# Two-block model on one core: the first block's attention output made by feature, with two steps moved

## The chip, the core and the metric

The kernel runs on one core of one Trainium2 chip. The metric is the device time of one execution in microseconds, lower is better. The engines are named as in the profile: PE is TensorE (PEld its weight loads), DVE is VectorE, ACT is ScalarE, POOL is GpSimd, SP is the queue that fetches the weights.

## What is computed

A model of two blocks of two layers each over 256 tokens of width 1024. Only the two layers of the first block are touched, and in them the attention branch, whose weights come from a softmax over keys that an index score has picked:

```
def dsa_attention(q, k, v, qi, ki, wi):
    ...
        q_g = q_b.reshape(bsz, Q_BLOCK, A_KV_HEADS, group, A_HEAD_DIM)
        s = jnp.einsum('btngd,btknd->btngk', q_g, k_g).astype(jnp.float32) * scale
        s = jnp.where(valid[:, :, None, None, :], s, -jnp.inf)
        p = jax.nn.softmax(s, axis=-1).astype(v.dtype)
        o = jnp.einsum('btngk,btknd->btngd', p, v_g)
        return o.reshape(bsz, Q_BLOCK, A_WIDTH)
...
def rwkv7_time_mix(z, mu, w0, w_up, a0, a_up, g_up, k_k, k_a, r_k, ln_w, ln_b):
    ...
    kk = (kf * k_k.astype(f32)).reshape(hs)
    kk = kk * lax.rsqrt(jnp.maximum(jnp.sum(kk * kk, axis=-1, keepdims=True), 1e-24))
    ...
        sa = jnp.einsum('bhvk,bhk->bhv', state, ka_t)
        state = (state * w_t[:, :, None, :] + sa[..., None] * kb_t[:, :, None, :]
                 + v_t[..., None] * k_t[:, :, None, :])
```

The second function is a recurrence over time. The kernel works it in four chunks of 64 tokens, and for that needs the inverse of a triangular matrix for each chunk and head. A layer adds three gated branches (attention, a short convolution, the recurrence), projects them, and ends in a feed-forward part.

## The kernel before

Every matrix product with weights is made of three matmuls on rounded parts: ACT rounds a slab of 128x2048 weights into `w_high` (step `round`, L596), DVE subtracts to get `w_low` (step `split`, L978), and PE multiplies high by high, high by low and low by high (L1499 to L1501). There are three slabs and three pairs of parts, so slab u is rounded once the products of slab u-3 are done. A slab's work is a *unit*: `uc` 0 to 3 and `cb` 0 and 1 feed the convolution branch, `ga` and `gb` 0 to 3 the gates of the first two branches, `br0` the projection of the attention output, and so on in the order of `UNITS_A`. Between units each engine does the steps that `schedule_a` hangs on them. All engines walk the same list in order, each doing its own part of a step, and wait for each other by semaphores; there is no scheduler.

Attention goes by pairs of heads k = 0 to 3, spread over seven host units (`rz` 6, `uc` 0 to 3, `cb` 0 and 1): at host n come `scores` of pair n, `turn` of pair n-2 (six transposes of the exponentials through banks 5 and 6, copied out by ACT) and `pv` of pair n-3. `pv` multiplies the transposed exponentials as weights (128 columns) by 64 columns of values: six matmuls with tokens on the output's partitions, each of which the profile lists as two records, since they are in full f32. DVE divides by the softmax sums as it empties bank 7 (L1271, L1273). Later, behind unit `ga` 2, `post` 0 and 1 transpose the outputs to features by tokens in banks 6 and 7 (L1877), and ACT and DVE make the high and low part that `br0` needs, both reading the bank (DVE at L1281).

In the same stretch the recurrence is prepared. Behind `uc` 3 PE spreads the inverse of the keys' norm over the heads' rows (`kk_spread`, L1912) and DVE scales the keys (`kk_scale`, L1309), scans the decays (L1291) and, behind `cb` 0, makes the scaled keys (`keys`, L1325 to L1331). PE makes the chunks' Gram matrices (`chunk`, L1948) and DVE masks them (`mask`, L1344). From here a serial chain runs beside PE's gate units: ACT writes the diagonal blocks out (`blocks_out`, L893), POOL reads them and inverts them by 15 steps of two small tensor ops (`invert`, L2185 and L2187), writes the inverses (L2191), makes the off-diagonal part and shifts a bias (`off_diag` L2197, `bonus_shift` L2153), and then issues eight DMAs that bring the transposed inverses back (`blocks_in`, L2161); ACT issues eight for the inverses themselves (L902). The first product of `solve` 0 on PE (L1994), behind unit `gb` 3, waits for POOL's eight.

The arena is an SBUF buffer for everything between; `bank` is PSUM.

Of the kernel before, what the change touches and what calls it, by code (L numbers as in the profile page):

```python
# [11 lines left out]
F32 = mybir.dt.float32  # L12
F32R = mybir.dt.float32r
I32 = mybir.dt.int32
ALU = mybir.AluOpType
# [290 lines left out]
def stage_starts():  # L306
# [14 lines left out]
    dve_emptied3=10, dve_emptied4=6, dve_emptied5=10, dve_emptied6=8, dve_emptied7=6, exps=4, g_made=2,  # L321
# [4 lines left out]
    normed=4, off_diagonal=1, outputs_turned=2, products=84, qk_raw=6, queries_ready=1, rate_made=2,  # L326
    reset_made=1, rest_copied=18, rhs_made=4, rooted=1, rooted_sums=2, roped=6, row_kept=1, sa_made=4,
    scored=4, silu=22, solved=8, spread_made=4, squared=8, state=3, state_made=3, summed=8, summed_decay=2,
    tok_made=6, tokens_scaled=1, transposes_in=128, turned=8, u_made=3, up_scaled=22, weighted=4, x_high=12,
    x_ready=12, y_made=4, y_rooted=1, y_scale=1, y_squared=2, y_variance=1, ya_done=2, ya_high=2, yb_high=2,  # L330
    yb_ready=2, yc=2, yc_high=2, yc_ready=2, z_mixed=7,), "b": dict(
# [83 lines left out]
def schedule_a(first):  # L415
# [22 lines left out]
    for n, unit in enumerate(hosts):  # L438
        put(unit, *([("conv", n - 1)] if 1 <= n < 5 else []), *([("lora_inputs", 0)] if n == 2 else []))
        work = [(name, n - lag) for name, lag in (("pv", 3), ("turn", 2), ("scores", 0)) if 0 <= n - lag < 4]  # L440
        put(unit, *(work + [ROUND_NEXT] if unit == ("uc", 3) else [ROUND_NEXT] + work))
    amid(("uc", 3), ("lora", 0), ("kk_inverse", 0))
    put(("uc", 3), ("kk_spread", 0), ("kk_scale", 0), ("blend", 0), ("decay", 0), ("blended", 0))
# [224 lines left out]
def scalar_a(core, eng, line, stage):  # L668
# [159 lines left out]
    def post(n):  # L828
        eng.wait_ge(*sem("outputs_turned").next(eng))
        act(core.xh[:, 2 * n:2 * n + 2, :], heads(bank[6 + n], T), ACT.Copy, sem("ya_high"))  # L830
# [222 lines left out]
def vector_a(core, eng, line, stage):  # L1053
# [212 lines left out]

    def pv(k):
        eng.wait_ge(*sem("weighted").upto(k + 1))
        rden = core.small[:, RDEN_:RDEN_ + 4]
        line.settled()  # L1270
        did(eng.reciprocal(rden, core.small[:, DEN_ + 4 * (k % 4):][:, 0:4]))  # L1271
        line.settled()
        did(tt(flat(core, OS_, 4).rearrange("p (m c) -> p m c", m=2)[:, :, P * k:P * k + P].rearrange("p m (h d) -> p m h d", h=2),  # L1273
               bank[7][:, 0:T].rearrange("p (m h d) -> p m h d", m=2, h=2),
               rden.rearrange("p (m h) -> p m h", m=2).unsqueeze(3).broadcast_to([P, 2, 2, HD]), ALU.mult),
            sem("dve_emptied7"))

    def post(n):
        b = 6 + n
# [1666 lines left out]
```

## Time and profile before

| | us |
|---|---|
| median of 3 runs | 1671.35 |
| lowest and highest of the 3 | 1671.22, 1672.12 |
| the profiled execution's own time | 1670.61 |
| its span, first to last instruction | 1668.1 |
| PE busy in the span | 1654.6 |
| DVE busy | 1195.6 |
| ACT busy | 971.6 |
| POOL busy | 213.4 |

A row of the timeline gives start, length, engine, line, operation, what it writes and reads, partitions and columns, the number of records, and in square brackets how long the engine had been idle and who released it. The length of a merged PE row includes the time in which the last result leaves the array, so the pace is read from start to start.

### The profile page before, as it was taken

Reading aid. Unit: us, or ns where it says so; the run is one execution under the profiler, and the core shown is the slowest. Engines: PE = TensorE matmul, PEld = TensorE weight load, DVE = VectorE, ACT = ScalarE, POOL = GpSimd, SP = SyncE. Lnnn points to the kernel's source line nnn. Section 1 sums busy time; section 2 is a strip of 40 time slices with the busy share of each in tenths; the row PEclk is TensorE's granted clock in tenths of the full one; section 3 lists DMA queues with packets and bytes.
Section 4 is the critical chain, followed back from the end, with each engine's and each line's share of the span. In section 5 each row is a group of like instructions: output and inputs, shape, how many; then the busy total and the mean of one; then the engine's idle time right before and its main releaser. Section 6 shows DMA issues by size and latency. Waiting matters only on the chain.

```text
span 1668.1 us, 29334 instructions
## 1 busy us (share of the span) xinstructions
PE 1654.6 (99%) x12160; PEld 1473.4 (88%) x12160; DVE 1195.6 (72%) x1676; ACT 971.6 (58%) x1483; POOL 213.4 (13%) x208
## 2 busy tenths in 40 slices
PE   9999999999999999999999999999999999999998
PEld 6999999999998999999999998778788987788887
DVE  7877547798888975548888875767756657677564
ACT  7674525565567565345555564666774556657743
POOL 1764500000002945100000000000000100000000
PEclk9999999999999999999999999999999999999999
DMA  7443523454545424525454445334445553443451
GB/s 263 152 152 113 185 103 125 180 202 177 188 160 196 158 102 148 166 92 191 155 204 176 185 178 187 142 128 175 140 167 180 183 189 131 148 175 128 169 185 51
DMA packets 48195, 268.14 MB, mean 161 GB/s; under 512 B 13568, under 2 KB 14464, under 8 KB 16448
## 3 DMA queue, kind: packets, MB, share of 16 engines
q1 hardware_dynamic: 38160, 263.65, 44.0%
q10 hardware_dynamic: 9136, 1.58, 0.5%
q8 instruction: 96, 1.57, 0.4%
q0 software_dynamic: 768, 1.05, 0.2%
q14 instruction: 35, 0.29, 0.1%
HBM read 264.42 MB, written 1.84 MB: 160 GB/s over the span
## 4 chain that ended last, share of the span: by engine, by line
PE 58%; DVE 1%; DMA 0%; ACT 0%; POOL 0%; issue 0%; DVEq 0%; ACTq 0%
PE bank L2662 11%; PE bank L2664 11%; PE bank L2663 10%; PE bank L1499 4%; PE bank L1500 4%; PE bank L1501 4%; PE bank L1552 4%; PE bank L1554 2%; PE bank L2692 2%; PE bank L2680 1%; PE bank L2724 1%; PE bank L2711 1%; PE bank L1046 1%; PE bank L2702 0%; PE bank L1638 0%; PE bank L1996 0%
## 5 line engine op out<-in xcount | busy, mean ns | idle before, releaser
L978 DVE TENSOR_TENSOR w_low<-slab,w_high 128x2048 fp32r<-128x2048 f32 x249 | 577.8, 2330 | 200.4 <-ACT w_high L596 193.5
L596 ACT ACTIVATE w_high<-slab 128x2048 fp32r<-128x2048 f32 x249 | 470.2, 1896 | 115.8 <-PE bank L2664 71.8
L1499 PE MATMUL bank<-act,w_high 128*128 128x256 f32 (+1 forms) x1744 | 501.9, 288 | 0.9 <-DVE w_low L978 0.8
L1500 PE MATMUL bank<-act,w_high 128*128 128x256 f32 (+1 forms) x1744 | 493.2, 283 | 0.0
L1501 PE MATMUL bank<-act,w_low 128*128 128x256 f32 (+1 forms) x1744 | 493.1, 283 | 0.0
L1499 PEld LDWEIGHTS bank<-act,w_high 128*128 128x128 f32 (+1 forms) x1744 | 332.8, 191 | 10.8 <-issue 5.6
L1500 PEld LDWEIGHTS bank<-act,w_high 128*128 128x128 f32 (+1 forms) x1744 | 333.1, 191 | 0.9 <-issue 0.5
L1501 PEld LDWEIGHTS bank<-act,w_low 128*128 128x128 f32 (+1 forms) x1744 | 333.0, 191 | 0.0
L2662 PE MATMUL bank<-w_high,act 128*128 128x512 f32 x768 | 305.7, 398 | 0.0
L2664 PE MATMUL bank<-w_low,act 128*128 128x512 f32 x768 | 299.7, 390 | 0.0
L2663 PE MATMUL bank<-w_high,act 128*128 128x512 f32 x768 | 299.3, 390 | 0.0
L1552 PE MATMUL bank<-act,w_high 128*128 128x512 f32 x576 | 204.4, 399 | 0.0
L2217 POOL TENSOR_TENSOR arena<-arena 128x512 f32<-128x512 f32 x8 | 14.4, 1798 | 1286.6 <-ACT arena L621 1286.6
L2662 PEld LDWEIGHTS bank<-w_high,act 128*128 128x128 f32 x768 | 144.3, 188 | 31.9 <-issue 3.7
L2664 PEld LDWEIGHTS bank<-w_low,act 128*128 128x128 f32 x768 | 144.2, 188 | 31.0
L2663 PEld LDWEIGHTS bank<-w_high,act 128*128 128x128 f32 x768 | 144.4, 188 | 28.1
L672 ACT ACTIVATE arena<-bank 128x512 f32<-128x512 f32 (+4 forms) x158 | 77.2, 499 | 154.2 <-PE bank L1554 44.9
L1554 PE MATMUL bank<-act,w_low 128*128 128x256 f32 x576 | 161.8, 281 | 0.0
L1552 PEld LDWEIGHTS bank<-act,w_high 128*128 128x128 f32 x576 | 108.3, 188 | 26.1
L1554 PEld LDWEIGHTS bank<-act,w_low 128*128 128x128 f32 x576 | 108.9, 189 | 0.0
L2290 ACT ACTIVATE arena<-bank,small 128x512 f32<-128x512 f32 x80 | 54.9, 686 | 83.3 <-PE bank L2664 82.2
L1148 DVE SCALAR_TENSOR_TENSOR arena<-arena,vectors 128x255 f32<-128x255 f32 (+1 forms) x176 | 85.1, 483 | 12.4 <-ACT arena L672 3.6
(261 smaller groups left out, 1850.8 us busy)
## 6 DMA issues: line engine op xcount, KB each, us to landing
slab<-stream_a SPq DMA_DIRECT2D x143, 1024.0 KB, 4.8
slab<-stream_b SPq DMA_DIRECT2D x104, 1024.0 KB, 4.7
residual<-x_t SPq DMA_DIRECT2D x4, 256.0 KB, 6.2
slab<-stream_a ACTq DMA_DIRECT2D x2, 512.0 KB, 5.7
lora_weights<-lora SPq DMA_DIRECT2D x2, 512.0 KB, 7.5
out_t<-residual SPq DMA_DIRECT2D x4, 256.0 KB, 2.3
d_inverse<-arena POOLq DMA_DIRECT2D x2, 256.0 KB, 2.3
constants<-common SPq DMA_DIRECT2D x1, 384.0 KB, 9.1
```

Source lines behind the costliest of these rows:

```text
L596: line.did(eng.activation(core.wh[u % PARTS][:, 0:SLAB_WIDTH[u]], core.slab[u % SLABS][:, 0:SLAB_WIDTH[u]], ACT.Copy), core.sem("slab_high"))
L672: line.did(eng.activation(out, in_, func, **kw), tally)
L978: line.did(line.eng.tensor_tensor(core.wl[u % PARTS][:, 0:SLAB_WIDTH[u]], core.slab[u % SLABS][:, 0:SLAB_WIDTH[u]], core.wh[u % PARTS][:, ...
L1148: did(stt(out=out[:, lag:T], in0=src[:, 0:T - lag], scalar=col("conv", 2 * FT * tap + half * FT + j), in1=out[:, lag:T], op0=ALU.mult, op1 ...
L1499: eng.matmul(out, wh, xh, start=first, stop=False, skip_group_check=True)
L1500: eng.matmul(out, wh, xl, start=False, stop=False, skip_group_check=True)
L1501: return eng.matmul(out, wl, xh, start=False, stop=last, skip_group_check=True)
L1552: eng.matmul(out[:].rearrange("p (n t) -> p n t", n=2), wh[:, k, j, :], core.x[:, :, at, :], start=k == 0, stop=False, skip_group_check=True)
L1554: return eng.matmul(out[:, 0:T], wl[:, k, j, :], core.xh[:, at, :], start=False, stop=k == 7, skip_group_check=True)
L2662: mm(bank[b][:], high, wh[:, k, :], start=(half == 0 and k == 0), stop=False, skip_group_check=True)
L2663: mm(bank[b][:], low, wh[:, k, :], start=False, stop=False, skip_group_check=True)
L2664: last = mm(bank[b][:], high, wl[:, k, :], start=False, stop=(half == 1 and k == 3), skip_group_check=True)
```

## The change

`pv` now uses the values as weights (64 columns) and lets the transposed weights of the softmax stream through, in a helper that the second block already uses (`pe_weighted`): four matmuls instead of six, with features on the output's partitions. Nothing has to be transposed afterwards, so PE has no `post` step any more. The division by the softmax sums can no longer be done on the output (tokens are now its columns), so DVE does it ahead of the transposes, on the exponentials, in a new step `share` (`dve_share`: a reciprocal of 128x4 and two multiplications in the arena, of 128x2x128 and 128x2x256), one host behind `scores`. `turn` waits for `shared` instead of `exps`. `pv` on DVE is a plain copy of 128x256, and `post` on ACT and DVE reads the arena instead of the banks. Two steps move: `kk_spread` goes ahead of `turn` 2 on PE, and at host `cb` 0 ACT does the copies of `turn` 3 ahead of rounding the next slab.

```diff
@@ schedule_a
-        work = [(name, n - lag) for name, lag in (("pv", 3), ("turn", 2), ("scores", 0)) if 0 <= n - lag < 4]
-        put(unit, *(work + [ROUND_NEXT] if unit == ("uc", 3) else [ROUND_NEXT] + work))
+        work = [(name, n - lag) for name, lag in (("pv", 3), ("turn", 2), ("scores", 0), ("share", 1)) if 0 <= n - lag < 4]
+        if n == 4:
+            work.insert(1, ("kk_spread", 0))
+        put(unit, *(work + [ROUND_NEXT] if n in (4, 5) else [ROUND_NEXT] + work))
...
-    put(("uc", 3), ("kk_spread", 0), ("kk_scale", 0), ("blend", 0), ("decay", 0), ("blended", 0))
+    put(("uc", 3), ("kk_scale", 0), ("blend", 0), ("decay", 0), ("blended", 0))
@@ ACT
     def post(n):
-        eng.wait_ge(*sem("outputs_turned").next(eng))
-        act(core.xh[:, 2 * n:2 * n + 2, :], heads(bank[6 + n], T), ACT.Copy, sem("ya_high"))
+        eng.wait_ge(*sem("outputs_kept").upto(2 * n + 2))
+        act(core.xh[:, 2 * n:2 * n + 2, :], core.a(OS_ + 2 * n, 2), ACT.Copy, sem("ya_high"))
@@ DVE
+    def share(k):
+        eng.wait_ge(*sem("exps").upto(k + 1))
+        dve_share(core, line, k, scores_of(core, k, ASC_), sem("shared"))
+
     def pv(k):
         eng.wait_ge(*sem("weighted").upto(k + 1))
-        rden = core.small[:, RDEN_:RDEN_ + 4]
-        line.settled()
-        did(eng.reciprocal(rden, core.small[:, DEN_ + 4 * (k % 4):][:, 0:4]))
-        line.settled()
-        did(tt(flat(core, OS_, 4).rearrange("p (m c) -> p m c", m=2)[:, :, P * k:P * k + P].rearrange("p m (h d) -> p m h d", h=2),
-               bank[7][:, 0:T].rearrange("p (m h d) -> p m h d", m=2, h=2),
-               rden.rearrange("p (m h) -> p m h", m=2).unsqueeze(3).broadcast_to([P, 2, 2, HD]), ALU.mult),
-            sem("dve_emptied7"))
+        did(eng.tensor_copy(flat(core, OS_ + k), bank[7][:, 0:T]), sem("dve_emptied7"))
+        line.tell(sem("outputs_kept"))
 
     def post(n):
-        b = 6 + n
-        eng.wait_ge(*sem("ya_high").next(eng))
-        did(tt(core.xl[:, 2 * n:2 * n + 2, :], heads(bank[b], T), core.xh[:, 2 * n:2 * n + 2, :].bitcast(F32), ALU.subtract),
-            sem(f"dve_emptied{b}"))
-        line.tell(sem("ya_done"))
+        low(2 * n, 2, core.a(OS_ + 2 * n, 2), "ya_high", "ya_done")
@@ PE
     def turn(k):
-        eng.wait_ge(*sem("exps").upto(k + 1))
+        eng.wait_ge(*sem("shared").upto(k + 1))
...
     def pv(k):
         eng.wait_ge(sem("act_emptied5").sem, turn.at[k])
-        p_t = turned_of(core, k, APT_)
         banks.fill(7, "dve")
-        for m in range(2):
-            for p in range(2):
-                for s in range(m + 1):
-                    n = 2 * m + p * (m + 1) + s
-                    ins = mm(bank[7][:, (2 * m + p) * HD:][:, 0:HD], p_t[:, n * P:n * P + P],
-                             half_of(core, WS_, s)[:, P + HD * p:P + HD * p + HD], start=(s == 0), stop=(s == m),
-                             skip_group_check=True)
-        ins.then_inc(sem("weighted").sem, 1)
-
-    def post(n):
-        if n == 0:
-            eng.wait_ge(sem("dve_emptied7").sem, banks.count[7, "dve"])
-        b = 6 + n
-        banks.fill(b, "dve")
-        for j in range(2):
-            for m in range(2):
-                ins = eng.transpose(bank[b][:, j * T + m * P:][:, 0:P], half_of(core, OS_, m)[:, T * n + P * j:][:, 0:P],
-                                    core.const("ident"))
-        ins.then_inc(sem("outputs_turned").sem, 1)
+        pe_weighted(eng, bank[7], turned_of(core, k, APT_),
+                    lambda t, p: half_of(core, WS_, t)[:, P + HD * p:P + HD * p + HD]).then_inc(sem("weighted").sem, 1)
```

PE at host `uc` 3, before: the last product of the unit, `pv` 1 (L1865), `turn` 2 (L1852), `kk_spread` (L1912), and the first product of `cb` 0.

```order
L1501 MATMUL bank<-act,w_low 128x256
L1865 MATMUL bank<-arena 128x64 x6
L1852 MATMUL bank<-constants,arena 128x128 x6
L1912 MATMUL bank<-arena,constants_a 128x256 x4
L1499 MATMUL bank<-act,w_high 128x256
```

The same place after the change (L1048 and L1051 are `pe_weighted`, L1890 is `kk_spread`, L1848 `turn`).

```order
L1497 MATMUL bank<-act,w_low 128x256
L1048 MATMUL bank<-arena 64x256 x2
L1051 MATMUL bank<-arena 64x128 x2
L1890 MATMUL bank<-arena,constants_a 128x256 x4
L1848 MATMUL bank<-constants,arena 128x128 x6
L1495 MATMUL bank<-act,w_high 128x256
```

Six matmuls have become four, and the spread stands ahead of the transposes.

DVE from the split of host `uc` 2 to the scan, before: L1303 inverts the keys' norms, L1187 empties `uc` 3's bank, then come `pv` 1, `kk_scale` (L1309), a small op for `blend` and the scan.

```order
L978 TENSOR_TENSOR w_low<-slab,w_high 128x2048
L1303 RECIPROCAL arena<-arena 128x256
L1187 TENSOR_TENSOR arena<-bank,arena 128x256
L1271 RECIPROCAL small<-small 128x4
L1273 TENSOR_TENSOR arena<-bank,small 128x2x128
L1309 TENSOR_TENSOR arena<-bank,arena 128x512 x2
L1313 TENSOR_SCALAR small<-vectors 128x4
L1291 SCALAR_TENSOR_TENSOR arena<-arena 128x1024
```

The same place after the change, with `share` 2 ahead of the split (L980) and `share` 3 (L1033, L1037) ahead of `kk_scale` (L1305).

```order
L1033 RECIPROCAL small<-small 128x4
L1037 TENSOR_TENSOR arena<-arena,small 128x2x128
L1037 TENSOR_TENSOR arena<-arena,small 128x2x256
L980 TENSOR_TENSOR w_low<-slab,w_high 128x2048
L1299 RECIPROCAL arena<-arena 128x256
L1189 TENSOR_TENSOR arena<-bank,arena 128x256
L1275 COPY arena<-bank 128x256
L1033 RECIPROCAL small<-small 128x4
L1037 TENSOR_TENSOR arena<-arena,small 128x2x128
L1037 TENSOR_TENSOR arena<-arena,small 128x2x256
L1305 TENSOR_TENSOR arena<-bank,arena 128x512 x2
L1309 TENSOR_SCALAR small<-vectors 128x4
```

Two multiplications inside the arena now stand between the copy of `pv` 1 and `kk_scale`.

DVE from the last masks to the gate units, before: masks, `keys` 1, a split, the two low parts of `post` (L1281), the splits of the next slabs.

```order
L1344 TENSOR_TENSOR arena<-bank,constants_a 128x512 x4
L1335 TENSOR_TENSOR arena<-bank,arena 128x512 x2
L978 TENSOR_TENSOR w_low<-slab,w_high 128x2048
L1281 TENSOR_TENSOR act<-bank,act 128x512 x2
L978 TENSOR_TENSOR w_low<-slab,w_high 128x2048 x6
```

After the change:

```order
L1340 TENSOR_TENSOR arena<-bank,constants_a 128x512 x4
L1331 TENSOR_TENSOR arena<-bank,arena 128x512 x2
L980 TENSOR_TENSOR w_low<-slab,w_high 128x2048
L1114 TENSOR_TENSOR act<-arena,act 128x512 x2
L980 TENSOR_TENSOR w_low<-slab,w_high 128x2048 x6
```

The order is the same; the two low parts now have both inputs in SBUF.

## Rows read from the trace of the kernel before

**Rows 1.** The page's busy time: us, share of the span, instructions.

```profile
PE 1654.6 (99%) x12160; PEld 1473.4 (88%) x12160; DVE 1195.6 (72%) x1676; ACT 971.6 (58%) x1483; POOL 213.4 (13%) x208
```

**Rows 2.** Waits of PE: us in total, times, longest.

```profile
PE bank L1877 <- ACT arena L672: 2.2, 2, 1.1
...
PE bank L1994 <- DMA arena<-d_inverse: 0.6, 1, 0.6
```

**Rows 3.** Timeline of PE in the first layer, host uc 2.

```profile
104.82 1.45 PE L1865 MATMUL bank<-arena 128*128 128x64 f32 x12
106.10 0.83 PE L1852 MATMUL bank<-constants,arena 128*128 128x128 f32 x6
```

**Rows 4.** Timeline of PE in the second block, the helper `pe_weighted` there.

```profile
1449.51 0.65 PE L1046 MATMUL bank<-arena 128*64 128x256 f32 x4
...
1450.31 0.66 PE L2738 MATMUL bank<-constants,arena 128*128 128x128 f32 x4
```

**Rows 5.** Timeline of PE in the first layer, from `post` 0 to unit ga 3.

```profile
163.03 0.60 PE L1877 MATMUL bank<-constants,arena 128*128 128x128 f32 x4
...
165.13 0.36 PE L1499 MATMUL bank<-act,w_high 128*128 128x256 f32 x1
```

**Rows 6.** Timeline of PE in the first layer, `solve` 0.

```profile
195.57 2.08 PE L1994 MATMUL bank<-arena 64*64 64x64 f32 x64 [0.55 <-DMA arena<-d_inverse]
```

**Rows 7.** Timeline of ACT and POOL: the chain's first DMAs and its last.

```profile
154.07 5.33 ACTq L893 DMA_DIRECT2D d_blocks<-arena  x8
...
185.89 4.50 POOL L2161 DMA_DIRECT2D arena<-d_inverse  x8
```

**Rows 8.** Timeline of DVE in the first layer, behind unit uc 3.

```profile
117.36 0.42 DVE L1187 TENSOR_TENSOR arena<-bank,arena 128x256 f32<-128x256 f32 x1 [3.46 <-ACT arena L672]
...
118.88 1.29 DVE L1309 TENSOR_TENSOR arena<-bank,arena 128x512 f32<-128x512 f32 x2 [0.36 <-PE bank L1912]
```

**Rows 9.** Timeline of DVE in the second block: both multiplications of one `dve_share`.

```profile
1053.80 1.02 DVE L1035 TENSOR_TENSOR arena<-arena,small 128x256 f32<-128x256 f32 x2
```

**Rows 10.** Timeline of POOL in the first layer: a free operation, and four of the chain.

```profile
142.62 2.23 POOL L2143 TENSOR_TENSOR arena<-arena,vectors 128x1024 f32<-128x1024 f32 x1
...
169.44 2.23 POOL L2185 TENSOR_TENSOR arena<-arena 128x64 f32<-128x64 f32 x1
171.75 0.32 POOL L2187 TENSOR_TENSOR arena<-arena 128x64 f32<-128x64 f32 x1
...
178.55 3.49 POOL L2197 TENSOR_TENSOR arena<-arena,constants_a 128x1024 f32<-128x1024 f32 x1
182.00 3.94 POOL L2153 TENSOR_TENSOR arena<-arena,vectors 128x1024 f32<-128x1024 f32 x1
```

**Rows 11.** Timeline of DVE, three of the splits beside that chain.

```profile
169.21 2.29 DVE L978 TENSOR_TENSOR w_low<-slab,w_high 128x2048 fp32r<-128x2048 f32 x1 [0.76 <-ACT w_high L596]
...
180.46 3.73 DVE L978 TENSOR_TENSOR w_low<-slab,w_high 128x2048 fp32r<-128x2048 f32 x1 [0.69 <-ACT w_high L596]
186.22 2.29 DVE L978 TENSOR_TENSOR w_low<-slab,w_high 128x2048 fp32r<-128x2048 f32 x1 [2.02 <-ACT w_high L596]
```

**Rows 12.** Timeline of ACT, a gate's sigmoids ahead of a rounding.

```profile
183.54 0.84 ACT L672 ACTIVATE arena<-bank,vectors 128x256 f32<-128x256 f32 x2 [3.11 <-PE bank L1501]
```

**Rows 13.** L2161's DMAs issued from 187 to 188, and from 189 on.

```profile
DMA to landing us min/median/max: 2.4/2.6/3.0
...
DMA to landing us min/median/max: 5.7/5.8/5.8
```

**Rows 14.** Busy time of stretches at the kernel's end; PEclk is the granted clock.

```profile
1659.00:1660.00 1.00, 1.00 (x11) 1.00 (x10) 0.00 (x0) 0.81 (x3) 0.00 (x0) 1.00 0.00 0
...
1661.00:1662.00 1.00, 0.40 (x1) 0.41 (x2) 0.51 (x3) 0.00 (x0) 0.00 (x0) 0.50 0.00 0
```

**Rows 15.** Timeline of PE: the opening burst, and the same shape later.

```profile
1.31 7.25 PE L2077 MATMUL bank<-arena 128*128 128x512 f32 x12 [1.31 <-POOL arena L2226]
...
154.59 1.98 PE L1931 MATMUL bank<-arena,constants 128*128 128x512 f32 x4
```

More of the change, by code:

```diff
@@ L320 @@
     convolved=22, decay_made=2, decays=1, diagonal=2, dve_emptied0=20, dve_emptied1=10, dve_emptied2=19,
-    dve_emptied3=10, dve_emptied4=6, dve_emptied5=10, dve_emptied6=8, dve_emptied7=6, exps=4, g_made=2,
+    dve_emptied3=10, dve_emptied4=6, dve_emptied5=10, dve_emptied6=7, dve_emptied7=5, exps=4, g_made=2,
     gate_input=1, gathered=3, hidden=22, hidden_high=22, hidden_low=22, index_scores=4, index_summed=4,
@@ L325 @@
     lora_out=2, masked=1, maxed=4, mean_square=2, mix_high=4, mix_ready=4, newest_tap=22, norm_spread=2,
-    normed=4, off_diagonal=1, outputs_turned=2, products=84, qk_raw=6, queries_ready=1, rate_made=2,
+    normed=4, off_diagonal=1, outputs_kept=4, products=84, qk_raw=6, queries_ready=1, rate_made=2,
     reset_made=1, rest_copied=18, rhs_made=4, rooted=1, rooted_sums=2, roped=6, row_kept=1, sa_made=4,
[L328 to L331, printed above, removed]
+    scored=4, shared=4, silu=22, solved=8, spread_made=4, squared=8, state=3, state_made=3, summed=8,
+    summed_decay=2, tok_made=6, tokens_scaled=1, transposes_in=128, turned=8, u_made=3, up_scaled=22,
+    weighted=4, x_high=12, x_ready=12, y_made=4, y_rooted=1, y_scale=1, y_squared=2, y_variance=1, ya_done=2,
+    ya_high=2, yb_high=2, yb_ready=2, yc=2, yc_high=2, yc_ready=2, z_mixed=7,), "b": dict(
     act_emptied0=9, act_emptied1=8, act_emptied2=7, act_emptied5=16, act_emptied6=17, act_emptied7=16,
@@ L1401, in vector_a @@
                                norm=norm, tables=tables,
-                               norm_x=lambda _: normed("norm"), lows=lambda _: lows(8), x_ffn=x_ffn, unit=unit, ki_turn=ki_turn, isc=isc, topk=topk, scores=scores, pv=pv, post=post,
+                               norm_x=lambda _: normed("norm"), lows=lambda _: lows(8), x_ffn=x_ffn, unit=unit, ki_turn=ki_turn, isc=isc, topk=topk, scores=scores, share=share, pv=pv, post=post,
                                decay=decay, kk_sum=kk_sum, kk_inverse=kk_inverse, kk_scale=kk_scale, blend=blend, blended=blended, keys=keys, mask=mask, solve=solve, scan_y=scan_y, gn=gn, ffn=ffn))
@@ L2068, in tensor_a @@
     walk(SCHEDULE[stage], dict(begin=begin, unit=unit, sum=sums, spread=spread_row, norm_x=norm_x, ki_turn=ki_turn, turns=turns,
-                               isc=isc, scores=scores, turn=turn, pv=pv, post=post, lora=lora, kk_sum=kk_sum, kk_spread=kk_spread, keys=keys,
+                               isc=isc, scores=scores, turn=turn, pv=pv, lora=lora, kk_sum=kk_sum, kk_spread=kk_spread, keys=keys,
                                chunk=chunk, tok=tok, solve=solve, scan_rhs=scan_rhs, scan_sa=scan_sa, scan_y=scan_y, gn=gn))
```

## The prediction

> **What bounds the kernel now.** The page's busy times come first: PE is busy for 99% of the span [rows 1], so over the whole kernel time is made of PE's work, and a matmul taken off PE should come off the end. The waits of PE come second, because they say where this is not so. They are short, but two lie in the stretch of this change [rows 2]: PE stands 1.1 us in each layer at the second group of output transposes, and 0.6 us in one layer at the first product of `solve`, released by a DMA that POOL issued. The second is the one to look at. It says that in the first layer PE reaches `solve` just ahead of a chain that runs beside it, at 195.57 [rows 6]. I then followed this chain backwards in the timelines of POOL, ACT and DVE: POOL issues its eight DMAs from 185.89 to 190.39; ACT began the chain's first DMAs at 154.07, released by the last mask [rows 7]. Between these points nothing waits for PE's gate units. So PE's time from the last mask to `solve` 0 is worth nothing if it shrinks: PE only waits longer there. What counts is when DVE ends the masks and how long POOL needs afterwards.
>
> **What PE gets back.** One old `pv` takes from 104.82 to 106.10, 1.28 us [rows 3]. The new form runs in the second block from 1449.51 to 1450.31, 0.80 us [rows 4]; I add 0.1 for the change of tile size, which that row's start already hints at, and take 0.9. Four in each layer: 4 x 0.38 = 1.5 us. The transposes of `post` and the wait between them go from 163.03 to 165.13, 2.1 us [rows 5]. Together 3.6 us in a layer, 7.2 in both. If PE set the end everywhere, that would be the result.
>
> **Where the chain starts.** DVE stands idle until 117.36, then goes to `kk_scale` at 118.88, and from there to the masks it hardly pauses [rows 8]. The old path has a reciprocal and a product between, 1.52 us from start to start. The new one has the copy (about as long as the product it replaces), the reciprocal, and both multiplications of `share` 3, which take 1.02 in the second block [rows 9]. PE's spread is earlier by its move and no longer the one waited for (0.36 was [rows 8]); so `kk_scale` comes about 0.5 later, while `pv` 2 and `pv` 3 lose a reciprocal each, about 0.2 apiece. Without anything else the masks end 0.1 late. But POOL convolves in that stretch, and the multiplications read two SBUF operands. Rows show what that means: a POOL operation that needs 0.32 took 2.23 when a split began just ahead of it at 169.21 [rows 10, 11], that is until the split's end, and the split of 180.46 took 3.73 instead of 2.29 because POOL was in its long operation until 182.04. Whoever comes second stands still. The shares before `uc` 3 meet POOL's convolutions as well. Bounds: 0.3 us earlier (no clash, and PE's gain passed on to ACT's sigmoids) to 1.5 later (each multiplication waits for a convolution step). I take 0.9.
>
> The Trainium skill (SBUF — State Buffer, section Who interferes with whom) says the same of such pairs: a DVE instruction with two SBUF inputs and a GpSimd instruction that reads SBUF lock each other out for a whole instruction, while a DVE instruction with only one SBUF input does not. By that rule, the trace agrees, and the move of `post` from PSUM to SBUF is what makes it block POOL.
>
> **How long POOL needs.** In its chain before, POOL lost 1.9 us to the split at 169.21 (2.23 less 0.32), 1.3 to the next (3.49 less 2.23, the length of such an operation when free) and 1.7 to the one of 180.46 (3.94 less 2.23); the split of 186.22 fell on DMA issues and cost nothing [rows 10, 11]. Now two things are added. First, the two low parts of `post` move from bank to arena: 0.69 each in such a form, half of a 1.3 us pair like that of [rows 8], right in the inversion. Cost 0 if they fall between POOL's steps, 1.3 if not; those steps follow each other closely, so 1.3. Second, the splits come earlier against POOL: ACT waited 3.11 us for PE ahead of the rounding of 184 [rows 12] and for shorter times ahead of the two before; with PE up to 3.6 us ahead, these waits go, while POOL is later by 0.9 and 1.3. Then the split of 186.22 meets POOL's computing instead of its DMA issues and costs up to 2.2, and the two before it cost full length, 0.9 and 0.5 more. Bounds 0 and 3.6; I take 2.6. POOL's last DMA is issued 0.9 + 1.3 + 2.6 = 4.8 us later.
>
> One thing gives back. DMAs issued from 187 to 188 landed after 2.6 us, those after 189 after 5.8 [rows 13], beside a slab whose load a split had just started. A later issue would find that load done: between 0 and 3.2 us back, I take 2.4. So `solve` 0 starts 2.4 later than before, at about 198, and PE, which arrives at 195.57 - 0.55 - 3.6 + (a wait for the scaled keys of about 0.9) = 192.3, idles for 5 to 6 us. Two layers: +4.8 us.
>
> **The clock.** PE has not stood still so long in this trace. At the kernel's end its granted clock was 1.00 in the slice from 1659, with narrow products running, and 0.50 from 1661, when it had stopped (columns: stretch, PE, PEld, DVE, ACT, POOL, clock) [rows 14]: 2.4 GHz fell to 1.2. What a fall costs I read from the opening burst: twelve records in 7.25 us, where the same shape later takes 1.98 for four, so 5.94 for twelve [rows 15], 1.3 us more. Bounds 0 (it stays up) and 2.0; I take 1.3 in each layer, 2.6.
>
> The Trainium skill (TensorE: Matmul & The Clock Gate, What's actually happening) says that low is the default and activity releases it; a stop of several microseconds in each layer would bring it back twice.
>
> **The sum.** 1670.61 + 4.8 + 2.6 = 1678.0 for the profiled execution. The median of the runs before is 0.7 above that execution's time, so I say 1678.5. Neither the ACT change at `cb` 0 nor the spread's move adds to it: the copies are hidden by the rounding that has until ga 1, the spread by PE's other work; without the former, `pv` 3, now earlier, would wait about 1 us, which the wait at `solve` would swallow too. `turn` 0 may wait up to 0.7 for `share` 0; that is also swallowed.
>
> **The rivals.**
> - *PE's gain arrives (faster).* The chain has slack, or is pulled along. For it: in the second layer PE hardly waits at `solve`, and the 5.8 us landings could shrink to 2.6 at once. Against: the 0.6 us wait of the first layer. All 7.2 us would give 1663.4 + 0.7 = 1664; with the landing alone (2.9 a layer), 1665.5. It decides where POOL's last issue is late by less than about 1 us.
> - *It cancels (no change).* The splits shift little, POOL is late by 2 to 3 us, the landing returns as much, and the clock holds: 1668 to 1674.5, say 1671.5. For it: each term on POOL is a matter of tenths in timing.
> - *Slower without the clock.* As forecast, but the clock holds: 1675.9.
> - *The rounding falls behind.* ACT waits for the written inverses before its own eight DMAs, then rounds br0's second slab; if POOL's write is very late, `br0` waits for its split: 1 to 3 us more, 1682. PE's own late start leaves it room.
>
> **How the numbers follow.** Slower with a fall of the clock 0.40 (1678.5), slower without it 0.15, rounding behind 0.05, cancelled 0.23, PE's gain arrives 0.17. Within 0.2% of 1671.35, about what a measurement of this kernel can tell from no change, is 1668.0 to 1674.7. So slower 0.60, same 0.23, faster 0.17. The range goes from 1668 (leaving the faster cases out) to 1684 (in one layer all upper bounds of the chain's delay, 1.5 + 1.3 + 3.6 with nothing back from the landing, in the other 2.4 as forecast, and 2.0 for the clock in each: 12.8 above 1671.35); given that it is slower, 1675 to 1682.
>
> **What would show it.** Waits of PE: none at transposes, and at the first product of `solve` 4 to 7 us in each layer, released by the DMA of the inverses. POOL: L2161's counterpart starts near 190 in the first layer, `off_diag` and `bonus_shift` above 2.23 or the inversion with three or more steps of over 2 us. DVE: `kk_scale` near 119.5 to 120.5. The granted clock at 0.5 behind both waits. The prediction is wrong if that wait stays under 2 us, or if POOL issues no later than 187.

## The result, and the profile after

The changed kernel takes 1677.11 us (median of 8 runs, 1676.20 to 1678.19) beside 1670.29 for the one before (8 runs): a ratio of 1.004, 95% interval 1.0031 to 1.0049, so 6.8 us slower. Its profiled execution took 1676.21 with a span of 1674.4 (before 1670.61 and 1668.1). PE's busy time fell by only 1.4 us, for a reason that comes below. The waits of PE in the changed kernel (us in total, times, longest):

```profile
PE bank L1972 <- DMA arena<-d_inverse: 8.9, 2, 5.4
...
PE bank L1926 <- DVE arena L1327: 0.8, 2, 0.4
PE bank L1048 <- DVE arena L1275: 0.6, 2, 0.3
PE bank L1848 <- DVE arena L1037: 0.4, 2, 0.2
```

The 2.2 us at the output transposes are gone, and 8.9 us stand at the first product of `solve` 0, where 0.6 stood [rows 2]. Three small waits are new: for the scaled keys, for bank 7, and for the shares. In PE's timeline both layers can be followed:

```profile
105.02 0.65 PE L1048 MATMUL bank<-arena 128*64 128x256 f32 x4
...
105.82 0.88 PE L1848 MATMUL bank<-constants,arena 128*128 128x128 f32 x6
...
192.18 0.28 PE L1497 MATMUL bank<-act,w_low 128*128 128x256 f32 x1
197.89 3.68 PE L1972 MATMUL bank<-arena 64*64 64x64 f32 x64 [5.43 <-DMA arena<-d_inverse]
201.50 0.39 PE L1495 MATMUL bank<-act,w_high 128*128 128x256 f32 x1
...
685.26 2.98 PE L1972 MATMUL bank<-arena 64*64 64x64 f32 x64 [3.44 <-DMA arena<-d_inverse]
688.17 0.58 PE L1495 MATMUL bank<-act,w_high 128*128 128x256 f32 x1
...
691.84 2.08 PE L1974 MATMUL bank<-arena 64*64 64x64 f32 x64
```

In the first layer PE arrives at 192.46 (197.89 - 5.43), 2.56 earlier than before (195.02), and starts 2.32 later [rows 6]. Its 64 records (32 products) take 3.61 us from start to start instead of 2.01. So the next unit begins 3.92 late. In the second layer `solve` 0 is 5.06 later than its counterpart of before (680.20), 1.14 more than came in from the first layer, and the second product group 6.57 later (685.27 before), 1.51 more. 3.92 + 1.14 + 1.51 = 6.57; the span grew by 6.3. Nothing outside this stretch adds to it. The clock (last number but two) in stretches around the two waits:

```profile
193.00:194.00 1.00, 0.00 (x0) 0.00 (x0) 0.00 (x0) 1.00 (x2) 0.00 (x0) 1.00 0.91 363
195.00:196.00 1.00, 0.00 (x0) 0.00 (x0) 1.00 (x1) 0.00 (x0) 0.00 (x0) 0.50 0.77 138
200.00:201.00 1.00, 1.00 (x24) 1.00 (x22) 0.00 (x0) 0.51 (x1) 0.00 (x0) 0.50 0.45 188
...
685.00:686.00 1.00, 0.74 (x24) 0.74 (x26) 0.38 (x1) 0.00 (x0) 0.00 (x0) 1.00 0.00 0
687.00:688.00 1.00, 1.00 (x24) 1.00 (x20) 0.00 (x0) 0.17 (x1) 0.00 (x0) 0.50 0.79 328
```

2.4 GHz became 1.2 in both layers, in the second only after PE had taken up work again. That is also why PE's busy time hardly fell: slow products are busy ones. Now the chain, POOL first (first layer):

```profile
164.29 1.30 POOL L2163 TENSOR_TENSOR arena<-arena 128x15 f32<-128x15 f32 x1 [1.05 <-DMA arena<-d_blocks]
...
168.00 0.64 POOL L2163 TENSOR_TENSOR arena<-arena 128x55 f32<-128x55 f32 x1
168.72 0.63 POOL L2165 TENSOR_TENSOR arena<-arena 128x55 f32<-128x55 f32 x1
...
170.20 2.26 POOL L2163 TENSOR_TENSOR arena<-arena 128x63 f32<-128x63 f32 x1
...
175.99 2.32 POOL L2163 TENSOR_TENSOR arena<-arena 128x48 f32<-128x48 f32 x1
...
178.76 2.20 POOL L2163 TENSOR_TENSOR arena<-arena 128x39 f32<-128x39 f32 x1
...
183.54 0.60 POOL L2169 DMA_DIRECT2D d_inverse<-arena  x1 [0.31 <-POOL arena L2167]
184.17 2.42 POOL L2175 TENSOR_TENSOR arena<-arena,constants_a 128x1024 f32<-128x1024 f32 x1
186.53 1.90 POOL L2131 TENSOR_TENSOR arena<-arena,vectors 128x1024 f32<-128x1024 f32 x1
188.45 4.51 POOL L2139 DMA_DIRECT2D arena<-d_inverse  x8
```

and DVE beside it:

```profile
118.85 2.00 DVE L1037 TENSOR_TENSOR arena<-arena,small 128x256 f32<-128x256 f32 x2
120.77 1.27 DVE L1305 TENSOR_TENSOR arena<-bank,arena 128x512 f32<-128x512 f32 x2
...
167.67 1.52 DVE L1114 TENSOR_TENSOR act<-arena,act 128x512 fp32r<-128x512 f32 x2 [2.16 <-ACT act L674]
170.00 2.29 DVE L980 TENSOR_TENSOR w_low<-slab,w_high 128x2048 fp32r<-128x2048 f32 x1 [0.81 <-ACT w_high L598]
175.88 2.29 DVE L980 TENSOR_TENSOR w_low<-slab,w_high 128x2048 fp32r<-128x2048 f32 x1 [3.60 <-ACT w_high L598]
178.55 2.29 DVE L980 TENSOR_TENSOR w_low<-slab,w_high 128x2048 fp32r<-128x2048 f32 x1 [0.38 <-ACT w_high L598]
183.65 6.94 DVE L980 TENSOR_TENSOR w_low<-slab,w_high 128x2048 fp32r<-128x2048 f32 x1 [2.81 <-ACT w_high L598]
```

Three splits, not one, now fall into the inversion, each with one POOL step of 2.2 to 2.3 us beside it that needs 0.3; the low parts of `post` cost two steps 0.33 us each. For this off_diag and bonus_shift run undisturbed (2.42 and 1.90 us instead of 3.49 and 3.94 [rows 10]), and the split that meets them is the one that stands: 6.94 us. When it ends, at 190.6, it frees a slab, whose load starts at once (SP's first of two in this row):

```profile
190.62 6.06 SPq L530 DMA_DIRECT2D slab<-stream_a  x2
```

How long POOL's DMAs took to land: in the first layer those issued up to 190.7 (five), those issued from 190.7 on (four, one of them in both), and in the second layer those from 680.5 on:

```profile
DMA to landing us min/median/max: 2.1/2.4/6.0
...
DMA to landing us min/median/max: 5.5/5.7/6.0
...
DMA to landing us min/median/max: 1.9/2.1/2.3
```

### The profile page after: what moved, and what is told of

The parts are those of the page before. It is cut to its first block, busy times and chain, and to the rows that moved or that the text cites. A ratio compares the mean times of both kernels' runs of the same rounds, so it can differ in the third digit from the quotient of the medians.

```text
span 1674.4 us, 29256 instructions
## 1 busy us (share of the span) xinstructions
PE 1653.2 (99%) x12112; PEld 1468.9 (88%) x12112; DVE 1208.0 (72%) x1692; ACT 972.1 (58%) x1483; POOL 211.1 (13%) x208
## 3 DMA queue, kind: packets, MB, share of 16 engines
HBM read 264.42 MB, written 1.84 MB: 159 GB/s over the span
## 4 chain that ended last, share of the span: by engine, by line
PE 56%; DVE 2%; ACT 1%; issue 0%; POOL 0%; DMA 0%; DVEq 0%; ACTq 0%
PE bank L2640 11%; PE bank L2642 10%; PE bank L2641 10%; PE bank L1548 4%; PE bank L1495 4%; PE bank L1496 4%; PE bank L1497 3%; PE bank L1550 2%; PE bank L2670 2%; PE bank L2658 1%; PE bank L2702 1%; DVE w_low L980 1%; PE bank L2689 1%; PE bank L1048 1%; ACT w_high L598 0%
## 5 line engine op out<-in xcount | busy, mean ns | idle before, releaser
L980 DVE TENSOR_TENSOR w_low<-slab,w_high 128x2048 fp32r<-128x2048 f32 x249 | 579.0, 2334 | 206.8 <-ACT w_high L598 199.2
```

Of the source, the lines that this page charges most:

```text
L980: line.did(line.eng.tensor_tensor(core.wl[u % PARTS][:, 0:SLAB_WIDTH[u]], core.slab[u % SLABS][:, 0:SLAB_WIDTH[u]], core.wh[u % PARTS][:, ...
```

## The experiments

My theory: PE's gain is real, but between the masks and `solve` 0 a chain of DVE, ACT, POOL and DMA sets the time; the change lengthens the chain and the longer wait then costs clock as well. Rivals: the loss is in DVE's new work or its order; the wait is a symptom and PE would wait elsewhere; the clock costs nothing of its own. All ratios are to the kernel before, run beside each kernel. The changed kernel's is 1.004. Each run's trace is of one execution, which need not be a typical one: its own time is given where it lies far from the median.

**1. POOL's bonus_shift later.** The last term of the schedule line moves behind `blocks_in`:

```diff
-    put(("gb", 0), ("off_diag", 0), ("bonus_shift", 0))
-    put(("gb", 2), ("blocks_in", 0))
+    put(("gb", 0), ("off_diag", 0))
+    put(("gb", 2), ("blocks_in", 0), ("bonus_shift", 0))
```

> The changed kernel, with POOL's bonus_shift (1.90 us at 186.53) moved from ahead of its eight DMAs of blocks_in to behind them. Theory (POOL's chain sets the first product of solve 0, and PE's saved time is only waited away there): the eight DMAs are issued 1.9 us earlier in each layer, solve 0 starts earlier by 1.9 in the layer where the landing follows the issue at once and by 0 to 1.9 where a slab load lies beside it; the wait of 8.9 us over both layers falls to 5 to 7, and the time from 1677.1 to 1673.3 (1675 if the landing gives nothing in layer 0). The clock still falls, since over 3 us of idle time remain in the first layer. Rival (the time is lost elsewhere, in DVE's shares or in the clock alone): the wait falls but the end stays at 1676 to 1678.

Measured: 1672.4 us (1669.93 to 1677.97 in 11 runs), ratio 1.002 (1.001 to 1.003): by the ratios 3.3 us less. The wait is 7.2 instead of 8.9 us, just above the 5 to 7 expected. In the first layer the DMAs went out only 1.0 earlier, since POOL now stood still for its own write:

```profile
187.46 4.50 POOL L2139 DMA_DIRECT2D arena<-d_inverse  x8 [1.21 <-DMA d_inverse<-arena]
```

**2. The same move in the kernel before** (same edit).

> The kernel before with the same move of bonus_shift, which takes 3.94 us there. Theory: the chain is relieved by up to 3.9 us, but PE arrives at 195.0 in layer 0 and just on time in layer 1, so only the wait of 0.55 us comes back, and little or nothing in layer 1: 1669.5 to 1670.0 beside 1670.3. Rival (the move is a gain by itself, through fewer clashes of DVE and POOL): as much as in the changed kernel, 1666 to 1668.

Measured: 1669.84 beside 1669.72, ratio 1.000 (0.9991 to 1.0008). The relief is worth something only where PE waits: the theory's first point holds.

**3. off_diag later too.**

```diff
+    put(("gb", 2), ("blocks_in", 0), ("off_diag", 0), ("bonus_shift", 0))
```

> The changed kernel with both long operations of POOL, off_diag (2.42 us) and bonus_shift (1.90 us), behind the eight DMAs. Theory: the DMAs are issued from 184.2 instead of 188.45; they land ahead of PE's arrival at 192.3 or within 1 us of it, off_diag ends at about 191; PE's wait falls from 8.9 to under 2 us over both layers, no fall of the clock, so 8 to 9 us of waiting and 3.1 of the slow clock less 0 to 2 come back: 1665 to 1668, faster than both kernels. Rival 1 (the landing is set by slab traffic, not by the issue): waits of 2 to 4 us in each layer stay, 1670 to 1674. Rival 2: off_diag, now last, becomes the one waited for; then PE's wait is put down to POOL, up to 1 us a layer.

Measured: 1671.74, ratio 1.0016 (1.0007 to 1.0025), no better than run 1. The forecast of 1665 to 1668 missed: I had expected 4.3 us of POOL's time on the path, and it was not there. POOL waits for its write to land instead, which takes 4.1 us in this first layer and 4.6 in the changed kernel's, so that the eight DMAs go out at 188.35, hardly earlier than the 188.45 of the changed kernel. Rival 1's time and waits came (5.6 us in two), though what was late was first of all the write, which that rival had not named. (The traced execution took 1674.60, near the slowest of the 11.)

```profile
183.92 0.60 POOL L2168 DMA_DIRECT2D d_inverse<-arena  x1 [0.31 <-POOL arena L2166]
188.35 4.47 POOL L2138 DMA_DIRECT2D arena<-d_inverse  x8 [3.83 <-DMA d_inverse<-arena]
```

**4. Fillers in the wait.** Ahead of the wait at `solve` 0 PE multiplies constants into bank 3:

```diff
+            for _ in range(160 if stage == "a0" else 96):
+                mm(bank[3][0:CH, 0:CH], core.const("ident")[0:CH, 0:CH], core.const("ident")[0:CH, 0:CH], ...)
             eng.wait_ge(*sem("transposes_in").upto(128))
```

> The changed kernel with extra products of 64x64 on a bank that nobody reads yet, issued by PE ahead of its wait at solve 0: 160 in layer 0 (5.0 us at the pace of 64 in 2.01 us) and 96 in layer 1 (3.0 us); they compute nothing that is used. They fill the idle time without removing it. Theory (the idle time and the lower clock are two separate costs): solve 0 starts as before, but takes 2.0 us instead of 3.6 and 2.9, and the granted clock stays at 1.00 behind it: 3.1 us less, 1674.0. Rival (the 64 products are slow for another reason, or the clock falls all the same): no change, 1677; or later where the filler is longer than the wait, by up to 0.5.

Measured: 1694.66. The filler was mis-sized, 17.6 us instead of 5.0. I had taken `solve`'s 64 records for 64 products, but each product is listed as two records; and mine took 0.11 us each, `solve`'s 0.063 (why, I did not test). Only this is usable: in both layers `solve` 0 behind the filler ran at a granted clock of 1.00, 63 of its 64 records in 2.03 us.

**5. The last share earlier.** `share` 3 leaves host `cb` 0's list for the middle of `uc` 3:

```diff
-    amid(("uc", 3), ("lora", 0), ("kk_inverse", 0))
+    amid(("uc", 3), ("lora", 0), ("kk_inverse", 0), ("share", 3))
```

> The changed kernel with the last share (share 3: reciprocal and two multiplications, 2.4 us with its waits at 118.64) ahead of the end of unit uc 3, where DVE stands idle for 2.10 us until 117.67. Theory (share 3 makes the chain start late): kk_scale comes at 118.5 to 119.5 instead of 120.77, the masks end 0.7 to 2 us earlier in each layer and POOL's inversion with them; solve 0 earlier by 0.5 to 2 us a layer: 1673 to 1676. Rival (the masks are bound by splits and PE's Gram matrices, not by DVE's start): kk_scale earlier, but the last mask still at 154 to 155, 1677.

Measured: 1675.71, ratio 1.0032 (1.002 to 1.0045), 1.3 us less than the changed kernel, within what the intervals leave open. The trace is clearer (its execution took 1677.19, the slowest of the five): both multiplications take 1.03 instead of 2.00 us, kk_scale starts at 118.60 instead of 120.77, the last mask ends at 153.58 instead of 154.69, and `solve` 0 of the first layer comes at 196.51:

```profile
115.90 1.03 DVE L1038 TENSOR_TENSOR arena<-arena,small 128x256 f32<-128x256 f32 x2
...
118.60 1.29 DVE L1306 TENSOR_TENSOR arena<-bank,arena 128x512 f32<-128x512 f32 x2
```

Half of the gain at kk_scale (2.17 us) arrives at the masks (1.11), and all of that at `solve` 0 (1.38). In the second layer nothing of it arrived: `solve` 0 stood at 685.46 though the DMAs went out 3.2 us earlier than in the changed kernel, because SP started a slab load at 678.42, between them, and they took up to 6.0 us to land (2.6 for those issued ahead of it).

**6. Fillers of the right size.** 45 and 27 products instead of 160 and 96.

> As the run with extra products, but with 45 of them in layer 0 and 27 in layer 1, since 160 took 17.6 us there, 0.11 us each: fillers of 5.0 and 3.0 us for idle times of 5.4 and 3.4. Theory (the lower clock costs on top of the wait): solve 0 starts when it starts in the changed kernel, takes 2.0 us from start to start, granted clock 1.00 behind it: 1674.0, that is 3.1 less. Rival (no separate price): 1677.

Measured: 1676.5, ratio 1.0033 (1.0021 to 1.0046). In the first layer the filler fits:

```profile
192.19 5.46 PE L1959 MATMUL bank<-constants 64*64 64x64 f32 x90
197.85 2.08 PE L1977 MATMUL bank<-arena 64*64 64x64 f32 x64 [0.21 <-DMA arena<-d_inverse]
202.93 2.08 PE L1979 MATMUL bank<-arena 64*64 64x64 f32 x64
```

`solve` 0 starts when it did, at 197.85, and the next product group comes 5.08 us later instead of 6.68: 1.60 us are the price of the clock in this layer, on top of the wait. In the second layer 1.72 us of idle time remained behind the filler and the granted clock fell to 0.50 all the same:

```profile
685.20 3.42 PE L1977 MATMUL bank<-arena 64*64 64x64 f32 x64 [1.72 <-DMA arena<-d_inverse]
```

This row also shows where the first layer's 1.60 us went: `solve` 0 starts at 685.20, as in the changed kernel (685.26), though POOL's eight DMAs went out 4.3 us earlier (from 675.10). A slab load that SP started at 677.34 lay between them, and they took up to 6.1 us to land. So one of the two prices was taken away and lost again at the next landing; the forecast of 1674.0 missed, and that the price counts to the end of the kernel is not shown by this run.

**7. Everything from solve on half a unit later.**

```diff
-    put(("gb", 3), ("solve", 0))
-    amid(("br0", 0), ("solve", 1))
...
+    amid(("br0", 0), ("solve", 0))
+    put(("br0", 0), ("solve", 1))
...
```

and so on to `gn` 2, in the middle of `gc` 3.

> The changed kernel with every step from solve 0 to gn 2 half a unit later, so that half of br0 0 (2.9 us of PE's work) stands ahead of solve 0; nothing is added or left out. Theory (the wait at solve 0 only swallows what PE has gained): 2.9 of 5.4 us of waiting are filled in layer 0, 2.9 of 3.4 in layer 1, and in layer 1 at least the clock holds; 5.8 us and 1.5 to 3.1 us of clock come back: 1668 to 1670, about the kernel before or faster. Rival (the scan's chain, now half a unit later, makes PE or ACT wait at its end, at gn 2 or br2): part of it or all is lost again, 1672 to 1677.

Measured: 1683.51, ratio 1.0077 (1.0063 to 1.0091), a clear miss. The waits:

```profile
PE bank L1890 <- DVE arena L1376: 8.1, 2, 4.1
PE bank L1972 <- DMA arena<-d_inverse: 3.6, 2, 2.0
```

5.3 us less at `solve` 0, and 8.1 new ones at gn 2's spread (L1890 is the helper that it shares with `kk_spread`), where PE never waited before: the recurrence behind `solve` has no slack for a half unit. The rival named for this run was right in kind, and too low with its 1677. So moving the recurrence by half a unit doesn't fill the wait; the runs below shorten the chain instead.

**8. The two moves undone.**

```diff
-        if n == 4:
-            work.insert(1, ("kk_spread", 0))
-        put(unit, *(work + [ROUND_NEXT] if n in (4, 5) else [ROUND_NEXT] + work))
+        put(unit, *(work + [ROUND_NEXT] if n == 4 else [ROUND_NEXT] + work))
```

with `kk_spread` back at the head of the list behind `uc` 3.

> The changed kernel without its two moves: PE's kk_spread behind turn 2 again, ACT's copies of turn 3 behind the rounding at cb 0. Theory (the moves add nothing that reaches the end): kk_scale waits for nothing more, since share 3 is what it waits for; PE waits about 1 us at pv 3 in each layer, and this is swallowed by the wait at solve 0: 1676.5 to 1678. Rival (the moves hold the loss down, or are part of it): over 2 us off 1677.1, to either side.

Measured: 1678.81, ratio 1.0049 (1.0036 to 1.0061), 0.8 above the range expected, but by the ratios not to be told from 1.004. PE waits 1.7 us more at `pv` and 1.2 more at `turn`, both for ACT, and 8.1 instead of 8.9 at `solve` 0.

**9. One slab behind the landings.** SP holds slab 29 of each layer back:

```diff
         eng.wait_ge(sem("slab_split").sem, u - SLABS + 1)
+        for stage in ("a0", "a1"):
+            if u == FIRST_SLAB[stage] + 29:
+                for name in ("transposes_in", "inverses_in"):
+                    eng.wait_ge(sem(name).sem, START[stage].get(name, 0) + 128)
         slab_to(core, eng, u)
```

> The changed kernel, but SP starts the load of one slab in each layer (number 29 of the layer) only when the sixteen DMAs that bring the inverses have landed. Theory (the 1 MB load falls between these small DMAs and holds the last of them up by 3.0 us in layer 0, where none lands between 194.3 and 197.3): solve 0 starts at 194.9 to 195.5 instead of 197.89; in layer 1, where the load was issued ahead of them, 0 to 1 us earlier; the slab itself is needed 8 us later and nobody waits for it. 3 to 4 us less, and up to 1.5 more if the clock holds: 1672 to 1674. Rival (the small DMAs are slow by themselves): landing as before, 1677. Second rival (the late slab is missed by ACT's rounding and PE's units): 1678 to 1681, with waits for w_low behind br0.

Measured: 1671.27, ratio 1.0006 (0.9997 to 1.0015). This one edit, which touches nothing of the change, takes away 5.7 of the 6.8 us, more than the 3 to 5 expected. All of POOL's DMAs in the first layer now land alike, and `solve` 0 starts 3.29 us earlier, at full clock (in the second layer PE waited 1.84 us, and there the clock fell):

```profile
DMA to landing us min/median/max: 2.0/2.2/2.4
```

```profile
194.60 2.08 PE L1976 MATMUL bank<-arena 64*64 64x64 f32 x64 [1.74 <-DMA arena<-d_inverse]
```

POOL issued at 188.65, no earlier than in the changed kernel (188.45).

**10. Three reliefs together**: 3, 5 and 9.

> The changed kernel with three reliefs of the chain together: share 3 ahead of the end of uc 3, off_diag and bonus_shift behind POOL's eight DMAs, slab 29 behind the landings. Theory (chain start, POOL's operations or its write's way back, and the slab together make the wait; PE's own gain of about 3 us a layer is real): POOL issues at 186.3 to 188 in layer 0, its DMAs land at 191 to 193, PE arrives at 191.5 to 192.5; waits of 0 to 1 us in each layer, no fall of the clock; 1665 to 1668. Rival (the scan behind solve, or the masks, set the end whatever PE does): solve 0 early, but new waits behind it, 1670 or more.

Measured: 1667.95, ratio 0.9986 (0.9977 to 0.9994), faster than both. In the first layer PE stood 2.82 us for off_diag, which had moved behind the DMAs and ended at 194.16 (191.80, 2.36 us); the DMAs had been there before it (the last was issued at 191.2, and none took over 2.4). The granted clock fell to 0.50 by the end of this wait, against the forecast, and the next product group came 6.32 us behind `solve` 0 instead of 5.08.

**11. The kernel before with reliefs 3 and 9.**

> The kernel before with the two of these reliefs that it can have (off_diag and bonus_shift behind the eight DMAs, slab 29 behind the landings). Theory (it was held by PE itself, with 0.55 us of waiting in layer 0 and none in layer 1): 0.5 to 1 us less, 1669 to 1670.5 beside its 1670 to 1671. Rival (the reliefs are worth as much without the change): as far below its own time as the relieved changed kernel is below 1677, 1660 to 1664.

Measured: 1669.44 beside 1670.2, ratio 0.9995 (0.9986 to 1.0004). Run 10's reliefs free the changed kernel of 9 us (1.004 to 0.9986); the two that the old one can have give it 0.8, not to be told from nothing. There PE itself was the bound: in the first layer it came to `solve` 0 at 194.49 and waited for nothing. What slab 29 held back gives there without the other relief was not run.

**12. The best version**: 1, 5, and 9 with slab 28 held back too.

```diff
-            if u == FIRST_SLAB[stage] + 29:
+            if u in (FIRST_SLAB[stage] + 28, FIRST_SLAB[stage] + 29):
```

> The changed kernel with share 3 ahead of the end of uc 3, bonus_shift alone behind POOL's eight DMAs (off_diag fits into the 4.26 us in which POOL waits for its own write to land, and was the last thing waited for when it stood behind them), and slabs 28 and 29 of each layer behind the landings, so that neither the write nor the reads share the queues with a 1 MB load. Theory: the write lands 2.4 us earlier in layer 0, POOL's DMAs are issued from 185, land by 190.5; PE finds them there at 191.5, no wait at solve 0 in layer 0, at most 0.5 us in layer 1, no fall of the clock: 1664 to 1666, about 2.5 less than with the three reliefs and 12 less than the changed kernel. Rival (two slabs late is one too many: rounding 28 or unit br0 waits for its slab): 1667 to 1671, with new waits of PE for w_low in br0 and br1.

Measured: 1664.96, ratio 0.997 (0.9959 to 0.9981): 5 us below the kernel before, 12 below the changed one. POOL's write lands after 2.3 us (4.6 in the changed kernel), and PE waits 0.45 us in one layer and 1.76 in the other (at most 0.5 was expected), both at full clock:

```profile
192.09 2.08 PE L1977 MATMUL bank<-arena 64*64 64x64 f32 x64 [0.45 <-DMA arena<-d_inverse]
...
675.34 2.08 PE L1977 MATMUL bank<-arena 64*64 64x64 f32 x64 [1.76 <-DMA arena<-d_inverse]
```

ACT's rounding of a late slab waited 2.0 us for its load in the first layer, but PE waited hardly longer for `w_low` than in the changed kernel (1.2 us against 1.1), so the rival did not come.

## Why the prediction was right, and where its terms were off

The forecast was 1678.5, the median is 1677.11; the forecast for the profiled execution was 1678.0, and it took 1676.21. The mechanism held, by runs 1, 2, 9 and 11: what PE gained was waited away at `solve` 0, and relieving the chain helps the changed kernel alone. Two of the signs named came out weaker than said: PE waited 3.44 us in the second layer, not 4 to 7, and POOL issued at 188.45 in the first, not near 190. So the chain's delay in the first layer was overrated, 4.8 us against 2.56, and that `solve` 0 was late there by nearly the 2.4 forecast (2.32) is in part luck. The terms, one by one:

- *What PE gets back.* 3.6 us a layer forecast. `pv` takes 0.80 (105.02 to 105.82), not 0.9, and the posts are gone; but PE reached `solve` 0 only 2.56 earlier, because it waits 0.9 a layer for shares, bank and keys. The 0.9 that had been counted for the keys alone (measured 0.4) stands for all three, so the arrival came as forecast (192.3, measured 192.46).
- *Where the chain starts.* 0.9 later forecast; ACT's DMAs behind the last mask start 0.7 later in the first layer (154.78 against 154.07) and 1.07 in the second (644.15 against 639.16, less the 3.92 that came in), POOL's first product of the inversion 0.74 and 1.6 (164.29 against 163.55, 653.86 against 648.34). The cause is as forecast: the two multiplications of share 3 took 2.00 us beside POOL's convolution and 1.03 when run 5 moved them. kk_scale came at 120.77, just past the 119.5 to 120.5 given.
- *The low parts of `post`.* 1.3 forecast, 0.66 measured in both layers. Two POOL steps stood for 0.33 us each: a low part of 0.69 us costs POOL only what is left of it when POOL's next short step comes.
- *The splits.* 2.6 forecast. POOL's last DMAs went out 2.56 later in the first layer; less start and low parts that is 2.56 - 0.74 - 0.66 = 1.2; in the second the DMAs went out 4.42 later (679.37 less 671.03, less 3.92), and 4.42 - 1.6 - 0.66 = 2.2. The losses before had been read off one free length, 2.23, from another operation; off_diag takes 2.42 and bonus_shift 1.90 undisturbed, so these lost 1.1 and 2.0 rather than 1.3 and 1.7, about the same sum. The step that failed is "the split of 186.22 meets POOL's computing instead of its DMA issues and costs up to 2.2": it met it, and in the first layer the split itself stood still, at no cost to POOL; in the second it cost POOL 1.26.
- *The landing.* 2.4 back forecast; the first layer gave 0.2 (solve 0 is 2.32 late, POOL's DMAs 2.56), the second 3.3 (1.14 and 4.4). The step "a later issue would find that load done" failed in the first layer for the same reason: the load starts when the split ends, and the split that POOL held up until 190.6 put it among the DMAs again. The second layer shows the other case: POOL waited, the split did not, and the load started at 675.34, 4.0 ahead of POOL's DMAs. So the errors of these two terms hang together: either POOL waits and the slab comes early, or the split waits and the slab comes late. The sum of all the chain's terms, 2.4 a layer, came out at 2.32 and 1.14; that the first is so close is luck, since start and low parts were wrong by 0.8 together on their own account.
- *The clock.* 1.3 a layer forecast from the opening burst; 1.60 and 1.51 measured. Run 6 shows in the first layer that it is a price of its own there, not what it is worth at the end of the kernel.
- *The moves at nothing*: run 8 agrees, and the wait of about 1 us at `pv` 3 without ACT's move came as said.

Sum forecast 4.8 + 2.6; measured 3.46 (2.32 + 1.14) + 3.1, to which 6.3 of span and 6.8 between the medians answer. Of the rivals, "it cancels" fell on the clock and on the first layer's landing; "PE's gain arrives" holds only with the chain relieved: run 12 against run 11 is 0.9970 against 0.9995, 4.2 us, of 7.2. That comparison isn't pure, since run 12 holds one slab more back and has bonus_shift alone behind.

How can a load from SP hold up DMAs from POOL? In the changed kernel's first layer the last four DMAs took 5.5 to 6.0 us, and 2.0 to 2.4 in run 9 with the 1 MB load behind them. The Trainium skill (DMA: Bandwidth & Descriptors, section Issuing engines are not separate DMA queues) says that transfers started by SP, ACT and POOL end up on the same 16 engines and interleave; the trace agrees that the queue they are issued from does not keep them apart, with 3.3 us between the two starts of `solve` 0. That they meet in these engines is the page's account; no run here isolates it.

What stays open: how POOL's and DVE's turns are decided in detail (below), why the runs of 1 spread over 8 us (1669.93 to 1677.97; a slab load on either side of the DMAs might do it, but only one execution was traced), and how much of the 2.2 us left in run 12 a further relief could take.

## What to carry to other kernels

A gain on the busiest engine is worth what the next meeting with a side chain leaves of it: look for the shortest wait (here 0.55 us) that names another engine or a DMA, and cost the change on that chain first. A wait that opens costs twice on the spot if the clock falls in it (1.60 and 1.51 us here). And before moving compute off a chain, look at what it covers: here the chain's own DMA round trip, while the large load beside the chain's small DMAs was the cheap thing to move.

## What the runs showed of the hardware that I had not expected

- *Who stands still, DVE or POOL, turned on 0.1 us.* In the second layer of the changed kernel the split began at 673.02, just ahead of POOL's DMA issue of 673.27, and POOL's off_diag behind that issue took 3.68 instead of 2.42:

```profile
673.02 2.29 DVE L980 TENSOR_TENSOR w_low<-slab,w_high 128x2048 fp32r<-128x2048 f32 x1 [2.42 <-ACT w_high L598]
```

```profile
673.27 0.60 POOL L2169 DMA_DIRECT2D d_inverse<-arena  x1 [0.30 <-POOL arena L2167]
673.89 3.68 POOL L2175 TENSOR_TENSOR arena<-arena,constants_a 128x1024 f32<-128x1024 f32 x1
```

  In the first layer the split began at 183.65, 0.11 us after that issue, and stood until POOL was through both operations. The same went for every split of runs 1, 4, 5, 6, 7, 9 and 12 that began 0.17 to 0.41 us after this issue with a long POOL operation next: 4.9 to 5.0 us with one behind it, 6.7 to 6.9 with two. One that began only 0.05 us after it, in run 12's second layer, went the other way: it took its 2.29 us, and off_diag 3.99.

```profile
664.78 2.29 DVE L985 TENSOR_TENSOR w_low<-slab,w_high 128x2048 fp32r<-128x2048 f32 x1 [2.73 <-ACT w_high L603]
```

```profile
665.35 3.99 POOL L2180 TENSOR_TENSOR arena<-arena,constants_a 128x1024 f32<-128x1024 f32 x1
```

  Where no operation followed (runs 3 and 10) the split took 2.29. The Trainium skill (SBUF — State Buffer, section Who interferes with whom) says that the order in which the two are issued decides who blocks. The second layer agrees: the split came first, and the 1.26 us that off_diag lost are about what was left of it (it ended at 675.31, 1.42 after off_diag's start). The first differs: the split is recorded ahead of off_diag, and it waited for two instructions of POOL, not one. Nor is that a rule: in the kernel before, the split of 180.46 began within off_diag and got its turn when that ended, ahead of bonus_shift [rows 10, 11].
- *The same idle time cost clock in one place and none in another.* 1.74 us (run 9, first layer) and 1.76 us (run 12) at `solve` 0 left the granted clock at 1.00; 1.84 us (run 9, second layer) and 1.72 us behind the filler (run 6) brought it to 0.50, in run 9 only after PE had begun again. A wait of this size has no fixed price here: 0, or 1.5 us (run 9) and 1.3 (run 6), by the time to the next product group, 6.56 and 6.42 us instead of 5.08.
